# Delta rule with row broadcasts by DMA for tiles 1 to 3, and an earlier square root in the output projections

## The chip, the core and the metric

The kernel runs on one core of a Trainium2 chip. The metric is the device time of one execution in microseconds (us). Five engines work side by side, each in the order of its own program: PE (matmuls), DVE (VectorE), ACT (ScalarE), POOL (GpSimd) and SP (here it only issues DMAs). They meet at semaphores.

## The reference, cut to what matters

The model is a two-layer decoder trunk on 512 tokens of width 1024: one gated-DeltaNet layer, one latent-attention layer, each followed by a mixture of 64 experts with a shared one. The change touches the delta rule of layer 0 and the output projection of both layers, with the norm and the router behind it. The core of the delta rule, per head and chunk of 64 tokens:

```python
g = jnp.cumsum(g, axis=-1)
decay = jnp.exp(jnp.where(incl, g[..., :, None] - g[..., None, :], -jnp.inf))
lower = jnp.where(strict, jnp.einsum('nbhid,nbhjd->nbhij', kb, k) * decay, 0.0)
sol = lax.linalg.triangular_solve(I + lower, rhs, left_side=True, lower=True, unit_diagonal=True)
attn = jnp.einsum('nbhid,nbhjd->nbhij', q, k) * decay
def step(S, inp):                       # scan over the chunks
    v_new = uc - wc @ S
    o = (qc * jnp.exp(gc)[..., None]) @ S + ac @ v_new
    S = S * jnp.exp(g_last)[..., None] + (kc * jnp.exp(g_last - gc)[..., None]).T @ v_new
# after the mixer, in each layer:
h = layer_norm(DN_ALPHA * h + mix, ln1_g[layer], ln1_b[layer])
scores = jax.nn.sigmoid(xf @ w_router)          # first step of the mixture of experts
```

## The kernel before, in words

The delta rule (the block `gdn_delta_rule`) goes over four tiles of 128 tokens, each two chunks. The eight heads are handled as two groups g of four; `s = 2*tt + g` numbers a group of a tile, and nearly all operations are on [128, 4 heads x 128].

For each tile the decay needs the summed gates in two shapes: as a column (one number per partition, `gcol`) and as a row (the same 128 numbers on all partitions). In the same way the weights need `k_gain` as a column and as a row. Rows are made on PE: `gate_rows` (L818) multiplies a broadcast column with the constant triangle `C_CUM`, and `gain_rows` (L837) multiplies a broadcast column with the identity; four matmuls for each group, into PSUM bank 0 or 4.

What happens to them: `decay_arg` (L1013, DVE) subtracts column from row; `decay` (L961, ACT) takes exp of the row twice (`eg_last`, `eg_row`), then abs and exp of the difference, which is `sym`; `upper_part` (L1144, POOL) masks `sym` into `upper`; `keys_queries` (L826, PE) makes key-key and query-key products, two halves for each group; `decayed` (L1018, DVE) multiplies them by `sym` and `upper`; `weighted` (L1028, DVE) multiplies by the gain row and then by the gain column. `diagonal` (L1138, POOL) writes the diagonal of gains into `diag`; `first_X` and `first_Y` (DVE) start the inverse from `diag` and the weighted products.

The triangular solve is an inverse in levels 0 to 4. In each, for both groups, PE makes `product` (L854) and, past level 0, transposes X (L864); ACT copies both to SBUF; PE makes `inverse` (L870); DVE subtracts the result from X. Within the levels of tile tt the rows and products of tile tt+1 are made: `gate_rows` in level 1, `keys_queries` in levels 2 and 3, `gain_rows` in level 4. `decay` of the next tile stands behind ACT's copies of level 2; the squares of the last tile's output (`out_squares`, L1057) stand on DVE behind `decay_arg` in level 1. After level 4 come `values_keys` (L884) and the scan over the tile's two chunks c (`from_state`, `from_values`). The prologue makes the rows and products of tile 0 in one go. Each block ends in a barrier of all engines.

The output projection (`mixer_out`, L1214) runs once in each layer. For each tile of tokens: PE projects, DVE adds the residual and takes the statistics, ACT takes the square root (`act_layer_norm`, L389), DVE normalises in two passes (L386, L387), PE transposes (`pe_rows`), ACT copies the transposed blocks (`act_rows`, L343), and PE computes the router's scores. ACT also rearranges the rows and stores them (`act_store_rows`, L350). The next block, the mixture of experts, begins on ACT with a sigmoid of the router's result (L2116).

Of the kernel before, what the change touches and what calls it, by code (L numbers as in the profile page):

```python
# [33 lines left out]
P = 128  # L34
# [78 lines left out]
def build(nc, a, out):  # L113
    ctx = ExitStack()
    with ctx:
# [14 lines left out]
        moe_sum = nc.dram_tensor("moe_sum", (T, D), F32).ap()  # L130

# [673 lines left out]

        with nc.Block(name="gdn_delta_rule") as block:
            @block.sync
            def _(sp):
                sp.dma_start(onorm[:, :], a["a_onorm_w"][0].rearrange("(p o) -> p o", o=1)).then_inc(onorm_in.sem, 16)

            @block.tensor
            def _(pe):
# [4 lines left out]

                def gate_rows(s):  # L818
                    tt, g, tok, b = tile(s)
                    if tt > 0:  # L820
                        pe.wait_ge(k_scaled.sem, k_scaled.base + s - 1)
                    for h in range(HG):
                        last = nc.tensor.matmul(b[0][:, h * P:(h + 1) * P], lhsT=g_tok[:, tt, HG * g + h:HG * g + h + 1].to_broadcast([P, P]), rhs=plane(C_CUM), start=True, stop=True)
                    last.then_inc(rows_ready.sem, 1)

                def keys_queries(s, half):  # L826
                    tt, g, tok, b = tile(s)
                    if tt > 0 and half == 0:
                        pe.wait_ge(sym_done.sem, sym_done.base + s + 1)
                    elif tt > 0:  # L830
                        pe.wait_ge(kq_done.sem, kq_done.base + ev(s, 0) + 1)
                    for j in range(2):
                        h = HG * g + 2 * half + j
                        last = nc.tensor.matmul(kq_bank(s, half)[:, 2 * j * P:2 * (j + 1) * P], lhsT=qkT[:, H + h, tok], rhs=qk_of[:, :, h, tok], start=True, stop=True)
                    last.then_inc(kq_ready.sem, 1)

                def gain_rows(s):  # L837
                    tt, g, tok, b = tile(s)
                    if tt > 0:
                        pe.wait_ge(kq_done.sem, kq_done.base + ev(s, 1) + 1)  # L840
                    elif g == 0:
# [52 lines left out]
                def from_state(s, c):  # L894
# [30 lines left out]
                for s in both(0):  # L925
                    gate_rows(s)
                for half in range(2):
# [4 lines left out]
                for tt in range(TT):  # L932
                    for level in range(LV):
# [26 lines left out]
            def _(act):  # L960
                def decay(s):  # L961
# [6 lines left out]
                    nc.scalar.activation(eg_last[:, tt % 2, g, :, :], heads(b[0][:, :])[:, :, CHUNK - 1::CHUNK], ACT.Exp)  # L968
                    nc.scalar.activation(eg_row[g][:, :, :], heads(b[0][:, :]), ACT.Exp)
# [7 lines left out]
                nc.scalar.activation(ecol[:, :, :, :], bank[3][:, 0:2 * TT * H].rearrange("p (a t h) -> p a t h", a=2, t=TT), ACT.Exp).then_inc(cols_exp.sem, 1)  # L977
                for s in both(0):
# [33 lines left out]
            def _(v):  # L1012
                def decay_arg(s):  # L1013
                    tt, g, tok, b = tile(s)
                    v.wait_ge(rows_ready.sem, rows_ready.base + s + 1)
                    nc.vector.tensor_tensor(sym[g], heads(b[0][:, :]), per_head(gcol[:, tt, HG * g:HG * g + HG]), ALU.subtract).then_inc(arg_done.sem, 1)
# [11 lines left out]
                def weighted(s):  # L1028
                    tt, g, tok, b = tile(s)
                    v.wait_ge(kq_done.sem, kq_done.base + ev(s, 1) + 1)  # L1030
                    v.wait_ge(b_ready.sem, b_ready.base + s + 1)
                    link(v, "dve", nc.vector.tensor_tensor(sym[g], heads(b_bank(s)[:, :]), S[tt % 2][g][:, :, :], ALU.mult))
# [45 lines left out]
                for tt in range(TT):  # L1078
                    for level in range(LV):
# [7 lines left out]
                        if level == 0:  # L1087
                            for s in both(tt):
# [38 lines left out]
            def _(pool):  # L1127
# [86 lines left out]
        def mixer_out(name, layer, mix_h, mix_l, w_hi):  # L1214
# [35 lines left out]
            with nc.Block(name=name) as block:  # L1250
# [64 lines left out]
                def _(act):  # L1315
# [4 lines left out]
                    for tt in range(TT):  # L1320
# [1158 lines left out]
        for c in (rows_ready, arg_done, sym_done, upper_done, b_ready, w_scaled, ktok_ready, k_scaled, uw_ready):  # L2479
# [133 lines left out]
```

## Time and profile before

| | |
|---|---|
| time, median of 3 runs | 2332.85 us (2330.3 to 2335.3) |
| the profiled execution's own time | 2327.69 us |
| its span | 2325.8 us |
| PE, DVE, ACT, POOL busy, share of the span | 92%, 66%, 56%, 20% |
| mean granted clock of PE, of full speed | 0.959 |
| the delta rule, first to last matmul | 251.2 to 473.5 us |
| end of the output projections, layer 0 and 1 | 551.2 and 1583.5 us |

The span is what the profiler saw of one execution; 1.9 us lie around it. Shares of busy time are means over stages that differ a lot, so the delta rule and the ends of the projections are to be read from their own stretches.

### The profile page before, as it was taken

What the parts mean: (1) busy time and instruction counts of PE and PEld (TensorE: products, weight loads), DVE (VectorE), ACT (ScalarE), POOL (GpSimd) and SP (SyncE); (2) the same over time, 40 slices, a digit from 0 to 9 for tenths busy, and PEclk for the clock granted to TensorE, in tenths of its full rate; (3) what the DMA queues carried; (4) which work ended last, traced back from release to release, by engine and by line L of the source; (5) the groups of instructions that cost most, each with busy time, mean ns of one, the idle gap of its engine ahead of it and who ended that gap; (6) DMA issues with size and microseconds to landing.
All of it is one profiled execution on the core that took longest, in us unless ns stands there. A gap on an engine that the chain in (4) does not pass through costs nothing. (4 is left out here: it accounts for less than half of the span.)

```text
span 2325.8 us, 35565 instructions
## 1 busy us (share of the span) xinstructions
PE 2130.4 (92%) x9937; PEld 1610.7 (69%) x9937; DVE 1542.8 (66%) x2548; ACT 1292.2 (56%) x2140; POOL 475.6 (20%) x367
## 2 busy tenths in 40 slices
PE   7998799999999999999995898998999999999993
PEld 6875688975677767777764745575776676777772
DVE  3762556665688777888774315556777777888884
ACT  3332233433577777777774222332677777777772
POOL 0000355400122222222221003000222222222220
PEclk9999899988999999999998897999999999999997
DMA  5221000004799999999997120026899999999993
GB/s 194 97 90 37 23 1 1 1 28 175 272 370 373 361 360 353 371 362 372 356 352 242 46 68 19 1 86 215 302 340 359 360 354 345 361 361 372 372 360 116
DMA packets 180098, 536.57 MB, mean 231 GB/s; under 512 B 26320, under 2 KB 57904, under 8 KB 180016
## 3 DMA queue, kind: packets, MB, share of 16 engines
q1 hardware_dynamic: 149968, 457.51, 52.3%
q0 software_dynamic: 25248, 69.25, 11.9%
q10 hardware_dynamic: 4800, 8.78, 1.0%
q8 instruction: 45, 0.74, 0.1%
q14 instruction: 37, 0.30, 0.0%
HBM read 501.50 MB, written 54.07 MB: 239 GB/s over the span
## 5 line engine op out<-in xcount | busy, mean ns | idle before, releaser
L1704 DVE TENSOR_TENSOR gu_l<-ring,gu_h 128x1024 fp32r<-128x1024 f32 x512 | 610.5, 1220 | 93.4 <-ACT gu_h L1590 82.9
L1590 ACT CAST gu_h<-ring 128x1024 fp32r<-128x1024 f32 x512 | 523.8, 1060 | 84.8 <-DMA ring<-in_moe_w_up 68.9
L1522 PE MATMUL bank<-gu_h,xgT_l 128*128 128x512 f32 x1024 | 412.8, 403 | 0.0
L1524 PE MATMUL bank<-gu_h,xgT_h 128*128 128x512 f32 x1024 | 401.5, 392 | 0.0
L1523 PE MATMUL bank<-gu_l,xgT_h 128*128 128x512 f32 x1024 | 400.5, 391 | 0.0
L1832 POOL DMA_INDIRECT xg<-h_rows,list_idx x128 | 147.3, 1151 | 911.6 <-issue 523.3
L1561 PE MATMUL bank<-ring,hmT_f 128*128 128x512 f32 x544 | 277.4, 591 | 0.0
L1597 ACT CAST down_h<-ring 128x1024 fp32r<-128x1024 f32 x130 | 136.1, 1047 | 229.9 <-DMA ring<-in_moe_w_down 141.9
L1710 DVE TENSOR_TENSOR down_l<-ring,down_h 128x1024 fp32r<-128x1024 f32 x130 | 159.2, 1225 | 113.0 <-ACT down_h L1597 111.5
L1851 POOL DMA_INDIRECT moe_sum<-y,out_idx x128 | 193.9, 1515 | 167.4 <-issue 144.6
L1524 PEld LDWEIGHTS bank<-gu_h,xgT_h 128*128 128x128 f32 x1024 | 193.0, 188 | 42.5
L1523 PEld LDWEIGHTS bank<-gu_l,xgT_h 128*128 128x128 f32 x1024 | 193.7, 189 | 37.2
L1522 PEld LDWEIGHTS bank<-gu_h,xgT_l 128*128 128x128 f32 x1024 | 193.7, 189 | 36.3
L1692 DVE TENSOR_TENSOR xgT_l<-bank,xgT_h 128x512 fp32r<-128x512 f32 x256 | 164.9, 685 | 43.8 <-ACT xgT_h L1580 35.1
L1558 PE MATMUL bank<-down_h,hmT_l 128*128 128x512 f32 x272 | 163.1, 600 | 6.4 <-DVE hmT_l L1697 6.4
L1496 PE MATMUL bank<-const,xg 128*128 128x128 f32 x1024 | 138.0, 279 | 23.4 <-DMA xg<-h_rows,list_idx 11.4
L1580 ACT CAST xgT_h<-bank 128x512 fp32r<-128x512 f32 x256 | 137.4, 595 | 19.3 <-DVE y L1718 15.6
L1496 PEld LDWEIGHTS bank<-const,xg 128*128 128x128 f32 x1024 | 115.4, 142 | 35.7 <-issue 32.0
L1561 PEld LDWEIGHTS bank<-ring,hmT_f 128*128 128x128 f32 x544 | 102.2, 188 | 23.3
L1534 PEld LDWEIGHTS bank<-const,hm 128*128 128x128 f32 x272 | 34.0, 141 | 111.3 <-DVE hm L1685 79.3
L1560 PE MATMUL bank<-down_h,hmT_h 128*128 128x512 f32 x272 | 106.9, 393 | 0.0
L1559 PE MATMUL bank<-down_l,hmT_h 128*128 128x512 f32 x272 | 106.9, 393 | 0.0
(353 smaller groups left out, 3416.6 us busy)
## 6 DMA issues: line engine op xcount, KB each, us to landing
ring<-in_moe_w_gate SPq DMA_DIRECT2D x256, 512.0 KB
ring<-in_moe_w_up SPq DMA_DIRECT2D x256, 512.0 KB
ring<-in_moe_w_down SPq DMA_DIRECT2D x256, 512.0 KB
ring<-in_a_w_in SPq DMA_DIRECT2D x32, 512.0 KB
ring<-in_a_w_out SPq DMA_DIRECT2D x8, 512.0 KB
h_rows<-ring ACTq DMA_DIRECT2D x8, 512.0 KB, 2.6
moe_sum<-y ACTq DMA_DIRECT2D x8, 512.0 KB, 6.8
ring<-moe_sum SPq DMA_DIRECT2D x8, 512.0 KB, 5.2
```

The costliest lines, as they stand in the source:

```text
L1496: last = nc.tensor.transpose(bank[2 + half][:, j * P:(j + 1) * P], xg[r % 2][:, k * P:(k + 1) * P], ident)
L1522: nc.tensor.matmul(out, lhsT=xl, rhs=wh, start=k == 0, stop=False)
L1523: nc.tensor.matmul(out, lhsT=xh, rhs=wl, start=False, stop=False)
L1524: last = nc.tensor.matmul(out, lhsT=xh, rhs=wh, start=False, stop=k == KD - 1)
L1558: nc.tensor.matmul(out, lhsT=xl, rhs=down_h[:, c], start=True, stop=False)
L1561: last = nc.tensor.matmul(out, lhsT=xf, rhs=ring[:, down_slot, CH + half * 512:CH + half * 512 + 512], start=False, stop=True)
L1590: nc.scalar.copy(gu_h[:, c, :, :], gate_up_cols(gate_slot, c * CH // 2, CH // 2)).then_inc(gu_hi.sem, 1)
L1692: nc.vector.tensor_tensor(xgT_l[:, r % 2, k, :], heads(bank[2 + half][:, :]), xgT_h[:, r % 2, k, :].bitcast(F32), ALU.subtract).then_inc(x ...
L1704: nc.vector.tensor_tensor(gu_l[:, c, :, :], gate_up_cols(gate_slot, c * CH // 2, CH // 2), gu_h[:, c, :, :].bitcast(F32), ALU.subtract).th ...
L1710: nc.vector.tensor_tensor(down_l[:, :], ring[:, down_slot, 0:CH], down_h[:, :].bitcast(F32), ALU.subtract).then_inc(down_lo.sem, 1)
L1832: pool.indirect_dma_start(out=middle_rows(xg[r % 2], n), out_offset=None, in_=h_rows, in_offset=bass.IndirectOffsetOnAxis(ap=list_idx[0:n, ...
L1851: pool.indirect_dma_start(out=moe_sum, out_offset=bass.IndirectOffsetOnAxis(ap=out_idx[0:n, r % 2:r % 2 + 1], axis=0), in_=middle_rows(y[r ...
```

## The change

Three things are changed.

1. The rows of tiles 1 to 3 no longer come from PE. In the prologue eight matmuls (`rows_of_all`) make the gate rows and the gain rows of all four tiles and eight heads once, on 8 partitions; ACT copies them to SBUF in two copies ahead of its first `decay`; SP stores them in a DRAM tensor `gain_row`, and then loads them, 256 KB at a time, broadcast to 128 partitions: gate rows into `upper[g]`, gain rows into `diag[g]` (twelve loads). DVE and ACT read the rows from there. `gate_rows` and `gain_rows` are gone from levels 1 and 4.
2. Waits follow from this. `keys_queries` of the next tile's first half waits for `k_scaled` (level 0) where it waited for `sym_done`, as it does not overwrite a row in the bank any more. `diagonal` on POOL waits for `w_scaled`, since `diag` holds the row until `weighted` has read it. `from_state` waits for the second half of `decayed`. In tile 0 the scaling of the keys waits for the stores, since the rows were copied into a buffer that it writes.
3. In `mixer_out` the square root of the last tile stands ahead of ACT's row copy and store of the tile before, and an added one-element sigmoid stands behind them, ahead of the last `act_rows`.

```diff
+                for kind, rows in enumerate((row_parts, row_parts2)):
+                    sp.wait_ge(row_copied.sem, row_copied.base + kind + 1)
+                    sp.dma_start(gain_row[kind].rearrange("t h q -> h t q"), rows).then_inc(row_stored.sem, 16)
+                sp.wait_ge(row_stored.sem, row_stored.base + 32)
+                for tt in range(1, TT):
+                    for s in both(tt):
...
+                        sp.wait_ge(kq_done.sem, kq_done.base + ev(s - 2, 1) + 1)
+                        sp.dma_start(upper[g], gain_row[0, tt, hs, :].partition_broadcast(P)).then_inc(gate_row_in[g].sem, 16)
+                    for s in both(tt):
...
+                        sp.wait_ge(xy_done.sem, xy_done.base + lev(s - 2, 0, LEVELS) + 1)
+                        sp.dma_start(diag[g], gain_row[1, tt, hs, :].partition_broadcast(P)).then_inc(gain_row_in[g].sem, 16)
...
+                def rows_of_all():
+                    for tt in range(TT):
+                        last = nc.tensor.matmul(bank[2][0:H, tt * P:(tt + 1) * P], lhsT=g_tok[:, tt, :], rhs=plane(C_CUM), start=True, stop=True)
+                    last.then_inc(row_made.sem, 1)
+                    for tt in range(TT):
+                        last = nc.tensor.matmul(bank[6][0:H, tt * P:(tt + 1) * P], lhsT=k_gain[:, tt, :], rhs=ident, start=True, stop=True)
+                    last.then_inc(row_made.sem, 1)
...
                     if tt > 0 and half == 0:
-                        pe.wait_ge(sym_done.sem, sym_done.base + s + 1)
+                        pe.wait_ge(k_scaled.sem, k_scaled.base + s - 1)
+                    elif tt == 0 and half == 1 and g == 0:
+                        pe.wait_ge(row_copied.sem, row_copied.base + 2)
...
-                        pe.wait_ge(w_scaled.sem, w_scaled.base + s + 3)
+                        pe.wait_ge(kq_done.sem, kq_done.base + ev(s + 2, 1) + 1)
...
-                            for s in both(tt + 1):
-                                if level == 1:
-                                    gate_rows(s)
-                                elif level < 4:
-                                    keys_queries(s, level - 2)
-                                else:
-                                    gain_rows(s)
+                            for s in both(tt + 1) if level in (2, 3) else ():
+                                keys_queries(s, level - 2)
...
+                for kind, (rows, b) in enumerate(((row_parts, bank[2]), (row_parts2, bank[6]))):
+                    act.wait_ge(row_made.sem, row_made.base + kind + 1)
+                    nc.scalar.copy(rows, heads(b[0:H, :])).then_inc(row_copied.sem, 1)
...
-                    nc.vector.tensor_tensor(sym[g], heads(b[0][:, :]), per_head(gcol[:, tt, HG * g:HG * g + HG]), ALU.subtract).then_inc(arg_done.sem, 1)
+                    if tt > 0:
+                        v.wait_ge(gate_row_in[g].sem, gate_row_in[g].base + 16 * tt)
...
+                    nc.vector.tensor_tensor(sym[g], upper[g] if tt > 0 else heads(b[0][:, :]), per_head(gcol[:, tt, HG * g:HG * g + HG]), ALU.subtract).then_inc(arg_done.sem, 1)
...
-                    link(v, "dve", nc.vector.tensor_tensor(sym[g], heads(b_bank(s)[:, :]), S[tt % 2][g][:, :, :], ALU.mult))
+                    link(v, "dve", nc.vector.tensor_tensor(sym[g], diag[g] if tt > 0 else heads(b_bank(s)[:, :]), S[tt % 2][g][:, :, :], ALU.mult))
...
-                        pool.wait_ge(xy_done.sem, xy_done.base + lev(s - 2, 0, LEVELS) + 1)
+                        pool.wait_ge(w_scaled.sem, w_scaled.base + s + 1)
...
+                            if tt == TT - 1:
+                                act_layer_norm(act, TT - 1, stats)
                             act_store_rows(act, tt - 1)
-                    act_layer_norm(act, TT - 1, stats)
+                    nc.scalar.activation(stats[0:1, 0, 15:16], eps_col[0:1, 0:1], ACT.Sigmoid)
```

PE's instructions in the prologue before: the gate rows (L823), the products (L834) and the gain rows (L845) of tile 0.

```order
793 L823 MATMUL bank<-const,g_tok 128x128 x8
794 L834 MATMUL bank<-qkT 128x256 x8
795 L845 MATMUL bank<-const,k_gain 128x128 x8
796 L861 MATMUL bank<-X,masked_0 128x128 x4
```

The same place after the change.

```order
793 L850 MATMUL bank<-const,g_tok 128x128 x8
794 L841 MATMUL bank<-const,g_tok 8x128 x4
795 L844 MATMUL bank<-const,k_gain 8x128 x4
796 L863 MATMUL bank<-qkT 128x256 x8
797 L872 MATMUL bank<-const,k_gain 128x128 x8
```

Eight matmuls with 8 output partitions stand between the gate rows and the products.

PE in levels 1 to 4 of tile 0 before, from the inverse of level 1; L861 is `product`, L867 the transpose, L879 and L881 `inverse`, L890 the first of `values_keys`.

```order
804 L879 MATMUL bank<-prod_vnew,Y 128x128 x8
805 L823 MATMUL bank<-const,g_tok 128x128 x8
806 L861 MATMUL bank<-X,masked_0 128x128 x4
...
810 L879 MATMUL bank<-prod_vnew,Y 128x128 x8
811 L834 MATMUL bank<-qkT 128x256 x4
...
822 L881 MATMUL bank<-Y,prod_vnew 128x128 x8
823 L845 MATMUL bank<-const,k_gain 128x128 x8
824 L890 MATMUL bank<-v_tok,Y 128x128
```

The same place after the change.

```order
806 L906 MATMUL bank<-prod_vnew,Y 128x128 x8
807 L888 MATMUL bank<-X,masked_0 128x128 x4
...
811 L906 MATMUL bank<-prod_vnew,Y 128x128 x8
812 L863 MATMUL bank<-qkT 128x256 x4
...
823 L908 MATMUL bank<-Y,prod_vnew 128x128 x8
824 L917 MATMUL bank<-v_tok,Y 128x128
```

The eight matmuls behind level 1 and the eight behind level 4 are gone; the same holds for tiles 1 and 2.

ACT at the end of the output projections before: L352 is the row copy, L353 its store, L391 the square root, L348 the copies of the transposed rows, L2116 the sigmoid of the next block.

```order
252 L348 COPY ring<-bank 128x4x128 x2
253 L352 COPY ring<-ring 128x1024
254 L353 DMA h_rows<-ring 128x1024
255 L391 ACTIVATE ln_stats<-ln_stats,eps_col 128x1
256 L348 COPY ring<-bank 128x4x128 x2
...
261 L2116 ACT_TABLE_LOAD
262 L2116 ACTIVATE scores<-bank 128x256
```

The same place after the change.

```order
253 L349 COPY ring<-bank 128x4x128 x2
254 L392 ACTIVATE ln_stats<-ln_stats,eps_col 128x1
255 L353 COPY ring<-ring 128x1024
256 L354 DMA h_rows<-ring 128x1024
257 L1368 ACT_TABLE_LOAD
258 L1368 ACTIVATE ln_stats<-eps_col 1x1
259 L349 COPY ring<-bank 128x4x128 x2
...
264 L2153 ACTIVATE scores<-bank 128x256
```

The square root has moved ahead of the copy and the store, and the table load from the next block to a place behind them.

## Rows read from the trace of the kernel before

**Rows 1.** Timeline of PE, tile 1: start, us, line, [idle before <- releaser].
```profile
340.48 2.11 PE L879 MATMUL bank<-prod_vnew,Y 128*128 128x128 f32 x16
343.69 1.13 PE L834 MATMUL bank<-qkT 128*128 128x256 f32 x4 [1.10 <-ACT ring L971]
...
346.39 1.05 PE L861 MATMUL bank<-X,masked 128*128 128x128 f32 x8
...
351.00 1.89 PE L834 MATMUL bank<-qkT 128*128 128x256 f32 x8
352.73 1.05 PE L861 MATMUL bank<-X,masked 128*128 128x128 f32 x8
...
357.33 1.95 PE L845 MATMUL bank<-const,k_gain 128*128 128x128 f32 x16
359.12 0.39 PE L890 MATMUL bank<-v_tok,Y 128*128 128x128 f32 x2
```

**Rows 2.** Timeline of PE, tile 0, level 2.
```profile
288.05 2.11 PE L879 MATMUL bank<-prod_vnew,Y 128*128 128x128 f32 x16
...
293.39 1.05 PE L861 MATMUL bank<-X,masked 128*128 128x128 f32 x8
```

**Rows 3.** Timeline of DVE, tile 1, level 1 into level 2.
```profile
336.24 0.69 DVE L1084 TENSOR_TENSOR X<-X,bank 128x512 f32<-128x512 f32 x1 [0.36 <-PE bank L879]
...
338.63 0.68 DVE L1062 TENSOR_TENSOR eg_row<-v_tok 128x512 f32<-128x512 f32 x1
...
341.60 0.68 DVE L1084 TENSOR_TENSOR X<-X,bank 128x512 f32<-128x512 f32 x1
```

**Rows 4.** Timeline of ACT, tile 1, decay of tile 2, first and last operation.
```profile
341.80 0.18 ACT L968 ACTIVATE eg_last<-bank 128x8 f32<-128x8 f32 x1 [0.48 <-DVE o_rms L1064]
...
344.74 0.63 ACT L971 ACTIVATE ring<-ring 128x512 f32<-128x512 f32 x1
```

**Rows 5.** Timelines of PE and ACT in the prologue.
```profile
253.48 3.62 PE L834 MATMUL bank<-qkT 128*128 128x256 f32 x16
...
268.32 2.08 PE L861 MATMUL bank<-X,masked 128*128 128x128 f32 x8 [9.44 <-DVE Y L1047]
...
253.58 0.18 ACT L968 ACTIVATE eg_last<-bank 128x8 f32<-128x8 f32 x1 [0.93 <-DVE ring L1016]
```

**Rows 6.** Timeline of DVE, first_X of tile 0, group 0 beside POOL, group 1 alone.
```profile
261.63 1.63 DVE L1041 TENSOR_TENSOR X<-ring,const 128x512 f32<-128x512 f32 x1
...
269.98 0.69 DVE L1041 TENSOR_TENSOR X<-ring,const 128x512 f32<-128x512 f32 x1
```

**Rows 7.** DMA issues: KB each, median us from issue to landing.
```profile
ln_gain<-in_ln_g SPq DMA_DIRECT2D x4, 512.0 KB, 4.0
```

**Rows 8.** Timelines of DVE, ACT and PE, end of the output projections of layer 0.
```profile
540.70 0.21 DVE L382 BATCH_NORM_AGGREGATE ln_stats<-ln_stats 128x2 f32<-128x12 f32 x1
...
540.06 2.07 ACT L352 COPY ring<-ring 128x1024 f32<-128x1024 f32 x1
...
542.53 0.29 ACT L391 ACTIVATE ln_stats<-ln_stats,eps_col 128x1 f32<-128x1 f32 x1 [0.40 <-ACT ring L352]
546.88 0.58 ACT L348 COPY ring<-bank 128x512 f32<-128x512 f32 x1 [4.05 <-PE bank L340]
...
539.74 2.00 PE L363 MATMUL bank<-ring 128*128 128x64 f32 x16 [0.23 <-ACT ring L348]
545.72 1.97 PE L340 MATMUL bank<-const,ring 128*128 128x128 f32 x8 [3.98 <-DVE ring L387]
547.51 3.68 PE L363 MATMUL bank<-ring 128*128 128x64 f32 x16
```

**Rows 9.** Timelines of ACT and DVE behind the barrier.
```profile
551.48 1.28 ACT L2116 ACT_TABLE_LOAD   x1 [1.19 <-PEq L1250]
...
556.31 0.42 DVE L1747 TENSOR_TENSOR biased<-scores,router_bias 128x256 f32<-128x256 f32 x1 [10.64 <-DMA router_bias<-in_moe_router_bias]
```

**Rows 10.** Timeline of PE, end of the output projections, layer 1.
```profile
1578.05 1.97 PE L340 MATMUL bank<-const,ring 128*128 128x128 f32 x8 [3.98 <-DVE ring L387]
```

More of the change, by code:

```diff
@@ L130, in build @@
         moe_sum = nc.dram_tensor("moe_sum", (T, D), F32).ap()
+        gain_row = nc.dram_tensor("gain_row", (2, TT, H, P), F32).ap()
         const = sb("const", [P, N_CONST, P])
@@ L804, in per_head @@
             return ap.unsqueeze(2).to_broadcast([P, HG, P])
+        row_parts = keg_wT[0][0:H, :, :]
+        row_parts2 = keg_wT[1][0:H, :, :]
+        row_made, row_copied, row_stored = after(convw_ready, 1), after(ab_ready, 1), after(const_in, 16)
+        gate_row_in, gain_row_in = [after(first_half_used, N_QKV), after(v_copied, H)], [after(hT_hi, 2 * TT), after(sums_ready, 2 * H + 1)]
         with nc.Block(name="gdn_delta_rule") as block:
@@ L838, in gain_rows @@
                     tt, g, tok, b = tile(s)
-                    if tt > 0:
-                        pe.wait_ge(kq_done.sem, kq_done.base + ev(s, 1) + 1)
-                    elif g == 0:
+                    if g == 0:
                         pe.wait_ge(cols_exp.sem, cols_exp.base + 1)
@@ L926, in _ @@
                     gate_rows(s)
+                rows_of_all()
                 for half in range(2):
@@ L967, in decay @@
                         act.wait_ge(rms_in.sem, rms_in.base + tt - 1)
-                    nc.scalar.activation(eg_last[:, tt % 2, g, :, :], heads(b[0][:, :])[:, :, CHUNK - 1::CHUNK], ACT.Exp)
-                    nc.scalar.activation(eg_row[g][:, :, :], heads(b[0][:, :]), ACT.Exp)
+                    rows = upper[g] if tt > 0 else heads(b[0][:, :])
+                    nc.scalar.activation(eg_last[:, tt % 2, g, :, :], rows[:, :, CHUNK - 1::CHUNK], ACT.Exp)
+                    nc.scalar.activation(eg_row[g][:, :, :], rows, ACT.Exp)
                     link(act, "act", nc.scalar.activation(sym[g], sym[g], ACT.Abs))
@@ L1014, in decay_arg @@
                     tt, g, tok, b = tile(s)
-                    v.wait_ge(rows_ready.sem, rows_ready.base + s + 1)
-                    nc.vector.tensor_tensor(sym[g], heads(b[0][:, :]), per_head(gcol[:, tt, HG * g:HG * g + HG]), ALU.subtract).then_inc(arg_done.sem, 1)
+                    if tt > 0:
+                        v.wait_ge(gate_row_in[g].sem, gate_row_in[g].base + 16 * tt)
+                    else:
+                        v.wait_ge(rows_ready.sem, rows_ready.base + s + 1)
+                    nc.vector.tensor_tensor(sym[g], upper[g] if tt > 0 else heads(b[0][:, :]), per_head(gcol[:, tt, HG * g:HG * g + HG]), ALU.subtract).then_inc(arg_done.sem, 1)
                 def decayed(s, half):
@@ L1030, in weighted @@
                     v.wait_ge(kq_done.sem, kq_done.base + ev(s, 1) + 1)
-                    v.wait_ge(b_ready.sem, b_ready.base + s + 1)
-                    link(v, "dve", nc.vector.tensor_tensor(sym[g], heads(b_bank(s)[:, :]), S[tt % 2][g][:, :, :], ALU.mult))
+                    if tt > 0:
+                        v.wait_ge(gain_row_in[g].sem, gain_row_in[g].base + 16 * tt)
+                    else:
+                        v.wait_ge(b_ready.sem, b_ready.base + s + 1)
+                    link(v, "dve", nc.vector.tensor_tensor(sym[g], diag[g] if tt > 0 else heads(b_bank(s)[:, :]), S[tt % 2][g][:, :, :], ALU.mult))
                     nc.vector.tensor_tensor(sym[g], sym[g], per_head(k_gain[:, tt, HG * g:HG * g + HG]), ALU.mult).then_inc(w_scaled.sem, 1)
@@ L1087, in _ @@
                         if level == 0:
+                            if tt == 0:
+                                v.wait_ge(row_stored.sem, row_stored.base + 32)
                             for s in both(tt):
@@ L2478, in build @@
         attended_l = sb("attended_l", [P, H, T], F32R, scope=att)
-        for c in (rows_ready, arg_done, sym_done, upper_done, b_ready, w_scaled, ktok_ready, k_scaled, uw_ready):
+        rows_ready.base += 2
+        b_ready.base += 2
+        for c in (arg_done, sym_done, upper_done, w_scaled, ktok_ready, k_scaled, uw_ready):
             c.base += NS
```

6 lines of the change are left out of this document (4 added, 2 removed).

## The prediction

> **What bounds the kernel now.** I read the shares of busy time first (PE 92%, DVE 66%, ACT 56%, POOL 20%), then PE's timeline through the delta rule, then those of DVE, ACT and POOL beside it, and last the ends of the two output projections. In the delta rule PE is the bound nearly everywhere between the prologue and the end. What the reader is to see in [rows 1] is that PE goes from piece to piece without idle time: the products of level 3 run into the next work, the gain rows (L845) into `values_keys` (L890). The only idle time that a row shows is ahead of `keys_queries`, 1.10 us, and ACT's `sym` ends it. So matmuls taken out of the levels should be worth their own length, as long as the engines that feed PE keep up. In the prologue it is otherwise: PE waits 9.44 us for DVE [rows 5], and whatever delays ACT's first `decay` delays all behind it. At the end of the projections PE waits 3.98 us for the norm [rows 8], in both layers [rows 10].
>
> **The change part by part.**
>
> *Rows out of levels 1 and 4.* Sixteen instruction halves for both groups occupy PE for 359.12 - 357.33 = 1.79 us [rows 1]; they last 1.95, so neighbours overlap by 0.16. The gate rows are the same count and form, so also 1.79. In each of tiles 0, 1 and 2 both go.
>
> *The wait for `sym` in level 2.* The inverse of both groups takes 2.11 - 0.16 = 1.95 us of PE [rows 1], one half of the products of the next tile 352.73 - 351.00 = 1.73. Without a wait, level 2's inverse to level 3's first product would thus be 3.68. In tile 0 it is 293.39 - 288.05 = 5.34 [rows 2], in tile 1 346.39 - 340.48 = 5.91 [rows 1]. The new wait, on `k_scaled`, was met a level earlier, so PE gets back 1.66 and 2.23.
>
> *What is late next.* In tiles 1 and 2 DVE also has the squares of the last output here. Before, it starts its second subtraction of level 1 at 336.24, the squares at 338.63, and its first subtraction of level 2 at 341.60, with nothing between [rows 3]. Operations of this size follow each other at some 0.60 us (0.69 less the overlap), so with the gate rows already in SBUF the two `decay_arg` stand at 336.84 and 337.44 and the squares at 338.04: 0.59 earlier, not 1.79. The subtraction then falls at 341.0 and ends at 341.7. PE's level 2 inverse starts at 340.48 - 1.79 = 338.69 and level 3 at 342.37, so the products of the next tile cover this. ACT's `decay` waits for the squares [rows 4]; it moves by the same 0.59 and ends at 344.74 + 0.63 - 0.59 = 344.8. Only then can ACT copy level 3's product and transpose, two copies of 0.6 us: about 345.9. PE would be ready for the inverse at 342.37 + (357.33 - 352.73 - 1.95) = 345.0. That is a new wait of 0.9 us a tile. In tile 0 there are no squares, and the same sum leaves no wait.
>
> Tile 0: 1.79 + 1.66 + 1.79 = 5.2. Tiles 1 and 2: 1.79 + 2.23 + 1.79 - 0.9 = 4.9 each. Together 15.0 us. From below, if DVE and ACT take all of the two row makings back as waits, 15.0 - 6 x 1.79 = 4.3; from above, if the new wait doesn't come, 16.8.
>
> *The prologue.* Eight matmuls with 8 output partitions stream the same 128 columns, so I take the same 1.79 us for them. They push the products from 253.48 to 255.3 [rows 5]. ACT makes two copies of 512 columns (0.58 each, by the row for such a copy [rows 8]); the second can start about 0.25 after its matmuls, at 255.5, and `decay` starts at 256.05 in place of 253.58: +2.5 us. From there to PE's first product of level 0 all is one chain through ACT, POOL and DVE. Bounds: 0, if the rows cost PE and ACT nothing, and +3.5, if both copies lie wholly behind the matmuls and the first product finds PE's clock low for a little longer.
>
> *The DMAs.* Two stores and twelve loads on SP, whose queue has nothing else here but one small load. A load of 512 KB broadcast to 128 partitions lands after 4.0 us [rows 7]; these have 256 KB. The gate rows of tile 2, say, are sent for when the second half of `decayed` of tile 1 is over (before 303 us) and are wanted at 336.8. The first, of tile 1, are sent for once the prologue has read `upper` (about 263) and wanted at 286.8. I cost them at 0; behind the wait on them DVE's subtractions queue, so a late one would cost what it is late, up to the whole. The wait on the stores in level 0 is met some 20 us earlier, 0.
>
> *POOL and DVE.* `diagonal` now waits for `weighted`, and so works while DVE handles the other group and, later, `first_X`. Beside a busy POOL such an operation of DVE took 1.63 us, alone 0.69 [rows 6]. The change also turns `decay_arg` and the first step of `weighted` into operations with two inputs in SBUF. If both steps of `first_X` were hit in three tiles and lay on the path, 6 x 0.94 = +5.6; below, 0. I take 0, because PE has `values_keys` and the state products to do between, and keep 5.6 for the range. The Trainium skill (SBUF — State Buffer, "Who interferes with whom") says that a DVE instruction with two SBUF inputs contends with a GpSimd instruction that reads SBUF, and that the one that comes second blocks fully. The pair in [rows 6] agrees in kind. By that rule the change adds 12 exposed operations where before there was a PSUM input; that is the slower rival below.
>
> *The square root.* The statistics of the last tile are ready at 540.70 + 0.21, the root starts at 542.53, behind the row copy (2.07) and its store [rows 8]. Moved ahead it starts at 541.0: 1.5 us earlier, and with it DVE's two passes and PE's transposes. The copy, the store (0.4), the table load (1.28, [rows 9]) and the one-element sigmoid (0.2) then fill ACT from 541.25 to 545.2; the transposed rows come at 546.88 - 1.5 = 545.4. It fits with 0.2 us to spare. Twice 1.5 = 3.0. Bounds 0 and 3.2 at PE's present clock.
>
> *The table load* saved behind the barrier: 0. DVE's first routing step starts at 556.31 and waits for the DMA of the router's bias, not for the scores, which were there at 553.2 [rows 9].
>
> The Trainium skill (ScalarE: Activation LUTs, "What ACT_TABLE_LOAD costs") puts a drain of about 1.38 us beside each switch, 2.66 in all. [rows 9] show 1.28 with the barrier ahead and no such drain. By that rule the filled wait would overrun by 1.2 us and leave 0.3 of the 1.5 in each layer, a total of 13.2 in place of 15.5.
>
> **The sum.** -15.0 + 2.5 - 3.0 = -15.5 us. On the profiled execution: 2327.69 - 15.5 = 2312.2. Its time is 5.2 below the median of the runs and below all three of them, so I put the change on the median: 2332.85 - 15.5 = 2317.3, say 2317. What lies behind, the experts, starts after a barrier each time and only shifts.
>
> **The rivals.**
>
> *The feeding engines take the room (smaller gain).* PE's idle time ahead of `keys_queries` shows that ACT is already late once a tile, and DVE's row of squares has no gap [rows 3]. Against it: at the other places no idle row of PE stands. With all six row makings back as waits: -4.3 + 2.5 - 3.0 = -4.8, 2328. Halfway, some 2323.
>
> *Contention turns it slower.* One mechanism: between level 4 and the state's update POOL is busy later than before, and DVE's operations with two SBUF inputs stretch by 0.94 each. In tiles 1 to 3 there are 6 `decay_arg`, 12 in `weighted`, 12 in `first_X`: 30 x 0.94 = 28 us, giving 2345. It decides from the 17th stretched operation that lies on the path (16 us). For it: [rows 6]. Against it: POOL is busy only 20% of the span, and PE has other work where these run.
>
> *PE's clock holds at the ends (more gain).* Behind the 3.98 us wait the router's 16 instructions take 3.68 us, where they took 2.00 a tile earlier [rows 8], the lower clock level by its ratio. With a wait of 2.5 us it may stay high: 1.7 in the router and 0.9 in the transposes, of which ACT's own copies and store give back about half. Some 1.3 a layer, -18, 2315. The other way round, a longer idle time in the prologue can leave the low level on for 1 to 2 us more.
>
> *The rows come late.* A landing 20 us longer than the row would be needed; I give it no weight of its own.
>
> **How the numbers follow.** Forecast, 2312 to 2322: 0.65. The clock holds or the new wait doesn't come, 2309 to 2315: 0.10. Half the gain is taken back by waits, contention or the overrun on ACT, 2322 to 2327: 0.13. All six row makings come back as waits, 2328 and about: 0.07. Slower by contention: 0.05. A measurement of this kernel tells about 0.2% (4.7 us) from no change, so faster means under 2328.2: 0.65 + 0.10 + 0.13 = 0.88; same 0.07; slower 0.05. The range 2310 to 2326 leaves out the last two cases and the outer edges.
>
> **What would show it.** Right: no idle time of PE ahead of `keys_queries` in level 2; a wait of some 0.9 us ahead of level 3's inverse in the tiles of level 2 with squares, ended by ACT; level 0's first product about 2.5 us later; the delta rule 12.5 us shorter; the last square root within 0.2 us of the statistics and the barrier 1.5 us earlier in both layers. Wrong: DVE idle on a DMA of `gain_row`; `first_X` at 1.6 us with PE idle behind it; ACT's table load ending after the transposes; the routing starting no earlier.

## The result, and the profile after

The changed kernel took 2308.9 us (median of 4 runs, 2305.9 to 2311.1) against 2332.3 (4 runs, 2330.3 to 2335.3): ratio 0.9897, 95% interval 0.9879 to 0.9915, or 23.4 us less. The forecast was 15.5 less, 2317, with a range from 2310 to 2326. Two later comparisons of the same pair on other chips gave 0.9936 (0.9916 to 0.9956) and 0.9904 (0.9882 to 0.9926). The single times of the two kernels in all comparisons together are 16 of the changed one with mean 2310.1 and 64 of the one before with mean 2329.9: 19.8 us less, with a standard error of 1.0 worked out from their scatter. Single runs of the kernel before lie between 2322.9 and 2337.3.

The profiled execution took 2311.05 us, its span is 2309.3 (before 2325.8): 16.5 less, where 15.5 had been worked out. The page shows 9857 matmuls in place of 9937 (96 taken out, 16 put in).

PE, tile 1, levels 1 to 3 of the changed kernel, from the timeline (start, us, line, [idle time before <- what ended it]); it answers to [rows 1]:

```profile
333.12 1.06 PE L888 MATMUL bank<-X,masked 128*128 128x128 f32 x8
...
335.78 2.11 PE L906 MATMUL bank<-prod_vnew,Y 128*128 128x128 f32 x16
337.73 1.89 PE L863 MATMUL bank<-qkT 128*128 128x256 f32 x8
339.46 1.05 PE L888 MATMUL bank<-X,masked 128*128 128x128 f32 x8
...
343.13 2.10 PE L906 MATMUL bank<-prod_vnew,Y 128*128 128x128 f32 x16 [0.85 <-ACT Y L1015]
```

`keys_queries` (L863) is one piece of eight without idle time; from the inverse of level 2 (335.78) to the first product of level 3 (339.46) it is 3.68 us, the sum made beforehand, where before it was 5.91. The new wait ahead of level 3's inverse is there, 0.85 us, and ACT ends it. PE's waits on ACT in the delta rule, whole stage; first the kernel before, then the changed one (line, what it waited for, us in total, times, longest):

```profile
PE bank L834 <- ACT ring L971: 4.5, 6, 1.1
```

```profile
PE bank L906 <- ACT Y L1015: 1.7, 2, 0.9
```

What is late next, from DVE's timeline of the changed kernel; it answers to [rows 3]:

```profile
333.32 0.69 DVE L1117 TENSOR_TENSOR X<-X,bank 128x512 f32<-128x512 f32 x1 [0.36 <-PE bank L906]
333.93 1.29 DVE L1046 TENSOR_TENSOR ring<-ring,gcol 128x512 f32<-128x512 f32 x2
335.13 0.68 DVE L1095 TENSOR_TENSOR eg_row<-v_tok 128x512 f32<-128x512 f32 x1
...
338.10 1.28 DVE L1117 TENSOR_TENSOR X<-X,bank 128x512 f32<-128x512 f32 x2
```

and ACT's, which answers to [rows 4]:

```profile
338.30 0.21 ACT L992 ACTIVATE eg_last<-ring 128x8 f32<-128x8 f32 x1 [1.68 <-DVE o_rms L1097]
...
341.40 0.63 ACT L995 ACTIVATE ring<-ring 128x512 f32<-128x512 f32 x1
```

The two `decay_arg` run together right behind the subtraction, neither waits for a DMA, and the squares follow them: ACT's `decay` waits for DVE's squares and not for a row.

The prologue, PE, ACT and SP; it answers to [rows 5]:

```profile
253.64 1.04 PE L841 MATMUL bank<-const,g_tok 128*8 128x128 f32 x8
254.52 1.04 PE L844 MATMUL bank<-const,k_gain 128*8 128x128 f32 x8
255.49 3.72 PE L863 MATMUL bank<-qkT 128*128 128x256 f32 x16
270.81 2.07 PE L888 MATMUL bank<-X,masked 128*128 128x128 f32 x8 [9.81 <-DVE Y L1080]
```

```profile
255.59 0.57 ACT L1004 COPY keg_wT<-bank 8x512 f32<-8x512 f32 x1 [0.30 <-PE bank L844]
256.08 0.16 ACT L992 ACTIVATE eg_last<-bank 128x8 f32<-128x8 f32 x1
```

```profile
255.32 1.15 SPq L817 DMA_DIRECT2D gain_row<-keg_wT  x2
262.17 0.95 SPq L824 DMA_DIRECT2D ring<-gain_row  x2
298.73 1.19 SPq L824 DMA_DIRECT2D ring<-gain_row  x2
```

The 16 instructions with 8 output partitions take 255.49 - 253.64 = 1.85 us (1.79 assumed); ACT starts `decay` at 256.08 (256.05 expected), and the first product falls at 270.81, 2.49 behind [rows 5]. SP sends for the gate rows of tile 2 at 298.7; DVE reads them at 333.9.

The end of the projections in layer 0, first ACT, then PE, then DVE behind the barrier; it answers to [rows 8] and, with the scores, to [rows 9]:

```profile
529.42 0.29 ACT L392 ACTIVATE ln_stats<-ln_stats,eps_col 128x1 f32<-128x1 f32 x1 [0.77 <-DVE ln_stats L383]
529.62 2.05 ACT L353 COPY ring<-ring 128x1024 f32<-128x1024 f32 x1
...
532.06 1.28 ACT L1368 ACT_TABLE_LOAD   x1 [0.39 <-ACT ring L353]
533.35 0.20 ACT L1368 ACTIVATE ln_stats<-eps_col 1x1 f32<-1x1 f32 x1
533.76 0.58 ACT L349 COPY ring<-bank 128x512 f32<-128x512 f32 x1 [0.21 <-PE bank L341]
538.38 0.38 ACT L2153 ACTIVATE scores<-bank 128x256 f32<-128x256 f32 x1 [1.19 <-PEq L1285]
```

```profile
532.61 1.97 PE L341 MATMUL bank<-const,ring 128*128 128x128 f32 x8 [2.39 <-DVE ring L388]
534.40 3.68 PE L364 MATMUL bank<-ring 128*128 128x64 f32 x16
```

```profile
542.65 0.42 DVE L1784 TENSOR_TENSOR biased<-scores,router_bias 128x256 f32<-128x256 f32 x1 [10.10 <-DMA router_bias<-in_moe_router_bias]
```

PE's wait has shrunk from 3.98 to 2.39 us. The root stands right behind the statistics; copy, store, table load and sigmoid end at 533.55, and ACT then waits 0.21 us for the transposed rows: everything fits, with the 0.2 to spare that was worked out. The sigmoid starts 0.01 us behind the end of the table load. The Trainium skill (ScalarE: Activation LUTs, "What ACT_TABLE_LOAD costs") adds a drain to each switch; here no row has room for one, and the sum without it was right. Behind the barrier the routing still starts with the router's bias.

Where the time went, by stages, as means over the profiles (four of the kernel before, three of the changed one; us):

| Stage | before | changed | difference | forecast |
|---|---|---|---|---|
| up to the delta rule | 250.9 | 251.0 | 0.0 | 0 |
| delta rule | 225.4 | 212.4 | -13.0 | -12.5 |
| from there to the barrier, layer 0 | 76.0 | 73.8 | -2.3 | -1.5 |
| experts, attention, to the barrier of layer 1 | 1030.8 | 1027.8 | -3.0 | -1.5 |
| to the end | 742.8 | 741.8 | -1.0 | 0 |
| span | 2326.0 | 2306.7 | -19.3 | -15.5 |

### The profile page after: what moved, and what is told of

Read it like the earlier page. It is cut to its first block and busy times, and to the rows that moved or that the text cites. A ratio compares the mean times of both kernels' runs of the same rounds, so it can differ in the third digit from the quotient of the medians.

```text
span 2309.3 us, 35424 instructions
## 1 busy us (share of the span) xinstructions
PE 2121.8 (92%) x9857; PEld 1603.3 (69%) x9857; DVE 1548.1 (67%) x2548; ACT 1293.9 (56%) x2144; POOL 485.6 (21%) x367
## 5 line engine op out<-in xcount | busy, mean ns | idle before, releaser
L1888 POOL DMA_INDIRECT moe_sum<-y,out_idx x128 | 198.7, 1553 | 172.6 <-issue 148.0
L1561 PEld LDWEIGHTS bank<-gu_h,xgT_h 128*128 128x128 f32 x1024 | 193.0, 189 | 42.5
L1598 PEld LDWEIGHTS bank<-ring,hmT_f 128*128 128x128 f32 x544 | 102.5, 188 | 23.4
```

Of the source, the lines that this page charges most:

```text
L1561: last = nc.tensor.matmul(out, lhsT=xh, rhs=wh, start=False, stop=k == KD - 1)
L1598: last = nc.tensor.matmul(out, lhsT=xf, rhs=ring[:, down_slot, CH + half * 512:CH + half * 512 + 512], start=False, stop=True)
L1888: pool.indirect_dma_start(out=moe_sum, out_offset=bass.IndirectOffsetOnAxis(ap=out_idx[0:n, r % 2:r % 2 + 1], axis=0), in_=middle_rows(y[r ...
```

## The experiments

**Changed kernel, again.** No edit.

> The changed kernel once more, unaltered. Theory A (my steps hold, and the rest of the 23.4 us is how executions of one kernel spread, since the profiled execution of before stood 5 us under its own median and that of the changed kernel 2 us above its own): ratio about 0.9925, near the 16.5 us by which the two spans differ; the profile again shows the first product of level 0 2.5 us later than before, the first transpose of the output projections 11.6 us earlier and the router's barrier of layer 0 13.1 us earlier. Theory B (a lasting gain that my steps do not hold, in the experts or the attention): ratio again 0.990, and a stage of the profile behind layer 0's router more than 5 us shorter than before.

Measured: 2312.4 us (6 runs) against 2327.8 (23 runs), 0.9936 (0.9916 to 0.9956): 15.4 less. The first comparison's 23.4 is not a size that repeats to the microsecond.

**The delta rule's edits alone.** The end of `mixer_out` as before.

```diff
-                            if tt == TT - 1:
-                                act_layer_norm(act, TT - 1, stats)
                             act_store_rows(act, tt - 1)
-                    nc.scalar.activation(stats[0:1, 0, 15:16], eps_col[0:1, 0:1], ACT.Sigmoid)
+                    act_layer_norm(act, TT - 1, stats)
```

> Only the delta rule's part of the change; the square root and the table load stand as before. Theory A: 11.5 to 12.5 us faster than before (0.995). Theory B with the gain tied to the new DRAM tensor or to the loads: some 18 to 20 us faster (0.992).

Measured: 2314.0 (6 runs) against 2327.8, 0.9942 (0.9921 to 0.9964). The delta rule has the length of the changed kernel (first product to the first transpose of its output 193.0 us, as there), and from there to the barrier it is 76.1 us, as before: PE waits 3.98 us for the norm again. The delta rule's edits carry most of the gain: 13.8 of the 15.4 us that the whole change has against the same runs.

**The output projection's edits alone.** The delta rule as before, the end of `mixer_out` as changed.

> Only the output projections' part: the square root of the last tile ahead of the row copy, the sigmoid's table loaded during the wait; the delta rule as before. Theory A: 3 us faster (0.9987), barrier 1.5 us earlier in each layer. Theory B with the gain tied to the table load or to when the experts' loads start: 6 to 10 us faster.

Measured: 2329.1 (12 runs) against 2327.8, 0.9999 (0.9985 to 1.0014). As a time this is inconclusive: the interval holds no change, and 3 us less (0.9987) as well. The profile shows them: PE's wait is 2.39 in place of 3.98. The stage takes 74.5 us to the barrier; it took 74.8 to 77.4 in four profiles of before, a scatter in which 1.5 us would not be seen.

**The kernel before, as a new run.** No edit; it is a yardstick for what such a comparison can tell.

> The kernel before, unaltered, timed against itself: how far executions of one kernel lie apart. Theory A: ratio 1.000 with single times from 2327 to 2335, and a profiled span that can lie several us off the median. Theory B: single times within 2 us and the span at its median, so that the 23.4 us are real in full.

Measured: 1.0016 (1.0001 to 1.0032) for a kernel against itself, 2331.1 (12 runs) to 2327.8. Its profile brought what the prediction lacked. PE in level 2 of tile 1, then the same stretch by windows (busy us of PE, weight loads, DVE, ACT, POOL, then the granted clock, DMA share, GB/s):

```profile
344.59 1.13 PE L834 MATMUL bank<-qkT 128*128 128x256 f32 x4 [1.10 <-ACT ring L971]
346.32 1.92 PE L834 MATMUL bank<-qkT 128*128 128x256 f32 x4 [0.60 <-ACT ring L971]
348.03 1.91 PE L861 MATMUL bank<-X,masked 128*128 128x128 f32 x8
```

```profile
344.00:348.00 4.00, 2.81 (x8) 2.02 (x9) 0.96 (x3) 2.24 (x5) 2.48 (x2) 0.81 0.01 2
```

In the execution that the prediction was made from, the waits end 0.9 us earlier. It has, in the same window:

```profile
344.00:348.00 4.00, 3.40 (x23) 2.86 (x22) 1.60 (x4) 1.86 (x5) 3.16 (x3) 1.00 0.01 2
```

Behind the same waits of 1.10 and 0.60 us PE was granted half its clock (1.2 in place of 2.4 GHz; "half clock" from here on) for some 3.4 us: the second four products took 1.92 in place of 1.13, the eight behind them 1.91 in place of 1.06. The same happened in tile 2, and at the border of tiles 0 and 1. The stage took 212.0 us from first product to transpose, where it had taken 207.1. In the run with the projection's edits alone it happened in tiles 1 and 2 (210.6).

**Changed kernel, a third time.** No edit, on another chip.

> The changed kernel once more, on whichever chip comes. Two comparisons so far: 4 executions against 4 gave -23.4 us, 6 against 23 gave -15.4. Theory A (sampling: executions of each kernel lie within some 12 us, and four against four fell on the far side): again some -15 to -17 us, ratio near 0.993, with the two intervals meeting. Theory B (it depends on the chip or the hour, with the change worth 23 us in one place): a ratio near 0.990 in at least one further comparison.

Measured: 2310.0 (6 runs) against 2331.2 (11 runs), 0.9904 (0.9882 to 0.9926), 21.2 less.

**The rows of all tiles made later in the prologue**, behind the products and gain rows of tile 0, ACT's copies behind the decays.

```diff
-                    elif tt == 0 and half == 1 and g == 0:
-                        pe.wait_ge(row_copied.sem, row_copied.base + 2)
...
-                rows_of_all()
...
+                pe.wait_ge(kq_done.sem, kq_done.base + 4)
+                rows_of_all()
```

> The eight matmuls that make the rows of all tiles move behind the prologue's other matmuls (once the second half of the decayed products has freed their banks), and ACT's two copies behind both decays. My theory of the prologue's +2.5 us (the copies stand ahead of ACT's decay): the first product of level 0 comes 2.5 us earlier than with the change, at the same place as before, the loads still land more than 10 us ahead of their readers, and the whole is 2 to 3 us faster than the changed kernel, 18 us faster than before. Rival (the later first product came from something else, or later rows arrive too late): first product unchanged, or DVE idle on a DMA in level 1 of tile 0.

Measured: 2309.8 (6 runs), 0.9903 (0.9881 to 0.9925), not to be told from the changed kernel. In the profile ACT's `decay` starts, and PE's first product with it, where they do in the kernel before:

```profile
253.05 0.18 ACT L991 ACTIVATE eg_last<-bank 128x8 f32<-128x8 f32 x1 [0.93 <-DVE ring L1045]
```

```profile
267.81 2.08 PE L886 MATMUL bank<-X,masked 128*128 128x128 f32 x8 [6.09 <-DVE Y L1079]
```

From the start of the stage (250.65) that is 17.16 us, against 19.57 in the changed kernel and 17.15 before. So the prologue's term is shown in the profile, cause and size: 2.4 us for rows ahead of the decays. It is too small for the times.

**The router's bias loaded a stage early.**

```diff
+                    sp.dma_start(router_biases[layer][:, :], a["moe_router_bias"][layer].partition_broadcast(P)).then_inc(bias_in.sem, 16)
```

> The changed kernel with the router's bias loaded in the block of the output projections, in both layers, where it came behind the barrier. The routing on DVE can then start with the scores, some 3.9 us earlier in layer 0 and 3 us in layer 1. Theory 1 (PE is busy with the shared expert until after the first gather has landed, so the routing is off the path): the routing starts 3 to 4 us earlier, the first gathered rows are transposed at the same time after the barrier, and the time stays within 1 us of the changed kernel. Theory 2 (the routing is the path behind the barrier): 6 to 8 us faster than the changed kernel.

Measured: 2312.8 (4 runs), 0.9916 (0.9888 to 0.9944). The routing now starts with the scores, 4.0 us earlier:

```profile
538.69 0.42 DVE L1786 TENSOR_TENSOR biased<-scores,router_bias 128x256 f32<-128x256 f32 x1 [6.31 <-ACT scores L2154]
579.42 1.04 PE L1535 MATMUL bank<-const,xg 128*128 128x128 f32 x8
```

PE's first transposes of gathered tokens stand at 579.42; in the changed kernel they stand at 580.26. Of the 4.0 us 0.8 is left there, and none in the time. Counted from the router's last matmul the first transposes come after 41.5 us, where they come after 42.2, 41.9 and 41.8 in the three profiles of the changed kernel, so 0.3 to 0.7 us is the better figure. So the saved table load is hidden twice, by the bias and by what lies between the routing and the experts.

**Both together.**

> Both of the last two edits together on the changed kernel. By my theories 2.5 us faster than the changed kernel by the prologue alone, some 18 us faster than before; by the rival on the routing some 24 us.

Measured: 2308.7 (6 runs, 2302.6 to 2317.5), 0.9911 (0.9886 to 0.9935). It has the shortest span of all profiles (2300.7) and the lowest median, but it can't be told from the changed kernel.

**The wait for `sym` put back**, in the changed kernel, all else left.

```diff
                     if tt > 0 and half == 0:
+                        pe.wait_ge(sym_done.sem, sym_done.base + s + 1)
                         pe.wait_ge(k_scaled.sem, k_scaled.base + s - 1)
```

> The changed kernel, with one wait put back: the next tile's first half of keys_queries again waits for sym_done, as before, besides k_scaled. Theory C (the part of the gain that my sum lacks is PE's clock: the waits of PE in level 2 of the kernel before are followed, in some executions, by a stretch at half the granted clock that costs 1.7 us each, and the profiled execution of before happened to have none): the waits of PE ahead of keys_queries come back, 0.5 to 1.1 us each, the stage from the first product of level 0 to the output projections grows from 193 us by 4 to 6 us of waiting, and low stretches behind those waits appear in part of the executions. About 5 to 8 us slower than the changed kernel. Rival D (the clock's stretches have nothing to do with those waits): 4 to 6 us slower, and no low stretch behind them in any profile.

Measured: 2321.9 (9 runs, 2319.0 to 2324.7) against 2329.1 (14 runs), 0.9968 (0.9956 to 0.9981). It keeps 7.2 us of the gain of 19.8 (4.4 to 10.2 by the interval), and so loses some 12.6 by this one wait, where the expectations were 5 to 8 and 4 to 6. PE, then the waits of the stage and two windows:

```profile
341.93 1.10 PE L864 MATMUL bank<-qkT 128*128 128x256 f32 x4 [2.47 <-ACT ring L996]
343.74 2.02 PE L864 MATMUL bank<-qkT 128*128 128x256 f32 x4 [0.70 <-ACT ring L996]
345.55 1.84 PE L889 MATMUL bank<-X,masked 128*128 128x128 f32 x8
```

```profile
PE bank L864 <- ACT ring L996: 7.3, 6, 2.5
```

```profile
344.00:348.00 4.00, 4.00 (x20) 3.64 (x20) 0.76 (x2) 0.58 (x2) 3.72 (x3) 0.60 0.01 2
396.00:400.00 4.00, 3.77 (x21) 3.44 (x22) 1.50 (x4) 0.77 (x3) 3.72 (x3) 0.70 0.00 0
```

With the gate rows' matmuls gone, PE comes to the wait earlier and stands there for 7.3 us in all, not 4.5. Both level 2 waits have a stretch of half clock behind them, and one more stands at the border of tiles 2 and 3. From first product to transpose it is 202.7 us against 193.0. Of the 9.7 us 7.3 - 1.7 = 5.6 are waits and some 2 x 1.7 the stretches in level 2: 9.0. The stretch at a border adds nothing, since the 193.0 have one too. The rest fits what a wait costs beside its idle time, because the work around it no longer runs as one piece: in tile 0, at full clock there, level 2's inverse to level 3's first product takes 5.54 us, 1.86 more than the 3.68 without a wait, for 1.38 us of idle time. The other 3 us of the time aren't located; the interval is as wide.

**The same, a second profile.**

> The same kernel, one more profile, to count low stretches of the granted clock behind PE's waits in level 2. Theory C: one or two in the tiles with squares, in at least one of the two profiles. Rival D: none.

Measured: the stage takes 202.8 us, with the clock at 0.60 and 0.70 in the same two windows. The waits of 2.5 us were followed by half clock in four cases of four. Its span is 6.0 longer than that of the run above (2326.1), with the same delta rule: that difference arose in the experts and the attention.

**The kernel before, two more profiles.**

> The kernel before, one more profile. Theory C: the stage from the first product of level 0 to the output projections takes 207.1 us plus 1.7 for each low stretch in it, most of them behind the waits of level 2; of three such profiles so far one had none, one two, one three. Rival D: the stretches lie elsewhere.

> The kernel before, a last profile for the same count. Theory C as in the look ahead of this one: 207 to 213 us for the stage, low stretches behind PE's waits of level 2.

Measured: 206.97 us in both, with the clock full in level 2. Of the five profiles of that delta rule three show no such stretch (207.1, 207.0, 207.0), two show it in both tiles (212.0, 210.6). So it is two executions of five rather than four independent cases of ten. Among the seven profiles of kernels without the wait (192.2 to 193.0 us) none has one in level 2; five have one at the border of tiles 1 and 2. Two of five against none of seven could be chance; with the long waits it is two executions of two.

## Why the prediction was right or wrong

**The mechanism of the delta rule was right, term by term.** Each tile from its first product to that of the next, before and changed in the profiled pair: tile 0 57.57 to 52.18, so -5.4 (forecast -5.2); tile 1 53.00 to 48.21, -4.8 (-4.9, with the new wait of 0.9, measured 0.85); tile 2 53.00 to 49.07, -3.9 (-4.9), and 48.20 in the third profile of the changed kernel. The 0.9 between those two is a stretch of half clock at the border of tiles 1 and 2:

```profile
371.19 3.87 PE L888 MATMUL bank<-X,masked 128*128 128x128 f32 x16 [0.37 <-DVE state L1154]
```

Tile 3 is 43.55 in both. The prologue cost +2.4, as forecast. Together the pair's delta rule is 11.7 shorter, where 12.5 was forecast. That the pair's spans still differ by 16.5, near the 15.5, is partly luck: its experts and attention came out 3.7 us shorter, where 1.5 was forecast, and that stage scatters by more.

**The rival of contention was seen, and lay off the path.** In the changed kernel, over tiles 1 to 3 (DVE by line, count, busy us, mean ns, idle time before):

```profile
L1075 DVE TENSOR_TENSOR X<-ring,X 128x512 f32<-128x512 f32 x6 | 9.8, 1640 | 0.2
...
L1066 DVE TENSOR_TENSOR ring<-ring,k_gain 128x512 f32<-128x512 f32 x6 | 6.3, 1052 | 0.2
...
L1046 DVE TENSOR_TENSOR ring<-ring,gcol 128x512 f32<-128x512 f32 x6 | 3.9, 685 | 0.0
```

Against before (1165 and 692 ns for the same steps) that is 2.9 and 2.2 us more on DVE, and nothing on `decay_arg`. The prediction named two ways to it: POOL is busy at a later time, and 12 operations get a second input in SBUF, `decay_arg` and the first step of `weighted` (L1065). Only the first came. None of the 12 was stretched, and in no `decay_arg` of tiles 1 to 3 was POOL at work. What was stretched, the second step of `weighted` (L1066) and `first_X`, had both inputs in SBUF before; new is that POOL's `diagonal` (L1177) and what follows it now run beside more of them. DVE and POOL behind level 4 of tile 0:

```profile
305.35 0.69 DVE L1065 TENSOR_TENSOR ring<-ring,S 128x512 f32<-128x512 f32 x1
305.51 1.42 POOL L1177 TENSOR_TENSOR ring<-const,k_gain 128x512 f32<-128x512 f32 x1 [8.57 <-DVE ring L1066]
306.07 1.41 DVE L1066 TENSOR_TENSOR ring<-ring,k_gain 128x512 f32<-128x512 f32 x1
```

None of it ends a wait of PE that was not there before; PE has the state's products to do. Of the 30 operations that the rival counted on, 12 were stretched (all six of the last step of `first_X`, three of its first step, three in `weighted`'s second step), and six of those in `first_X` had been before. The feeding engines took no row back either, but for the one wait that was forecast.

**The ends were right in kind.** Root and barrier came 1.5 us earlier. The rival that PE's clock holds there came true in part: in layer 1 the transposes behind the shorter wait start at full clock and take 1.2 to 1.4 us, not 1.97, in all three profiles of the changed kernel, though the router behind them is at half clock each time:

```profile
1561.58 1.16 PE L341 MATMUL bank<-const,ring 128*128 128x128 f32 x8 [2.40 <-DVE ring L388]
1563.04 3.67 PE L364 MATMUL bank<-ring 128*128 128x64 f32 x16 [0.30 <-ACT ring L349]
```

The router follows 1.46 us behind the start of the transposes in place of 1.80 (the wait before is in [rows 10]), 0.3 us earlier where the rival had 1.3, and in layer 0 nothing. That what lies behind the barrier "only shifts" was wrong in layer 1. From the router's last matmul to the first transposes of gathered tokens it is 41.5 to 41.7 us in the four profiles of before and 42.5 to 42.6 in the three of the changed kernel, since half clock now lasts 6 us behind that matmul in place of 4. It goes with the projection's edits: 42.5 with them alone, 41.6 with the delta rule's alone. Some 0.9 us of the 1.8 gained there is lost again. A slip in the prediction's own sum changes nothing: the overrun on ACT that it prices for the drain would leave 13.1 in total, not 13.2.

**What failed: the price of the wait for `sym`, and PE's clock, which the sum holds constant.** The step "PE gets back 1.66 and 2.23" read the wait from one execution in which nothing followed it. In two of five profiles PE's clock fell to half behind it in tiles 1 and 2, 1.7 us each time (the tile takes 54.67 in place of 53.00). The mean length of that stage before is therefore 208.7 us and not the 207.1 of the profile used, and the level term is -15.9 on the means of five and seven profiles (192.8 against 208.7), where it was -15.0 in the sum and -14.1 in the pair. Putting the wait back shows the mechanism with its sign: four stretches of four, in the same place, though behind longer waits.

This covers about 1 of the 4.3 us between the forecast of -15.5 and the -19.8 of all runs. More of it goes with the clock in the rest of the execution, for which the sum has no term. The record has the span and the mean granted clock of every run of these comparisons but four, and span x (1 - clock) is what half clock would cost if it always cost its full price. It is 98.8 us on average over 60 runs of the kernel before and 95.4 over the 16 of the changed one: 3.5 less, with a standard error of 1.0. Without it the spans are 2229.1 and 2213.0, so 16.1 less, with an error of 0.8, beside the forecast of 15.5. Among the 60 runs a microsecond of it goes with 0.7 us of span, so 2.4 to 3.5 of the 19.8 us go with the clock. This is an estimate from a correlation; only the part in level 2, 1.4 us of these, was put to a test by an edit.

**What is not explained.** Why the changed kernel spends less time at half clock outside level 2 stays open, and so do the 1 to 2 us that are left; the 19.8 itself has a standard error of 1.0. By the table of stages they lie in the projections and behind them, where single profiles of one kernel differ as much. The stage to the barrier took 77.4 and 74.8 us in two profiles of the kernel before, the longer one with half clock for 23 us in it and the shorter with 17. Experts and attention took from 1025.5 us, with 94 at half clock (both late edits together), to 1036.9, with 126 (the wait put back, second profile). The range was too narrow at its lower end, by 1.1 us in the first comparison: it had been made from the unknowns of the sum, around a median of three runs, and a comparison of a few runs of this kernel with a few others is itself unsure by some 4 us. That first comparison gave the largest gain of the three.

## What to carry to other kernels

A wait on PE costs its own length, a little for the broken run of work around it and, in some executions, half clock behind it; price it from several profiles, and count a wait removed as worth more than its row shows. When matmuls ahead of a wait are taken out, the wait grows by what they took, so moving the rows to DMA paid in full only because the wait went too. When an operation is stretched by a neighbour, look at which engine works beside it at that moment, and not only at where its inputs lie. Build a sum on a single profile if it is sound, but place it by the scatter of single runs, not by the interval of its own terms.

## What the runs showed of the hardware

- A wait of PE of 1.1 us and one of 0.6 us a little later were followed by about 3.4 us at half the granted clock in 4 of 10 cases (both tiles 1 and 2 in two of five profiles), the same program and the same waits each time; a wait of 2.5 us in 4 of 4; without a wait there, in 0 of 14. In level 2 such a stretch cost 1.7 us, at the border of two tiles 0.9, since PE otherwise waits 0.7 us there.
- A matmul of 128 columns with 8 output partitions takes as long as one with 128: 16 instructions in 1.85 us against 1.79.
- The 256 KB broadcasts from DRAM to 128 partitions landed a median of 3.2 us after their issue.
- ACT's table load took 1.28 us with nothing behind it: the next activation started 0.01 us later.
- A DVE operation of 128x512 f32 with both inputs in SBUF took 0.69 us with POOL idle and up to 1.74 beside it. In tiles 1 to 3: the last step of `first_X` 1.64 in six of six (POOL at work throughout), the second step of `weighted` 1.41 in three and 0.69 in the three with POOL idle, `decay_arg` 0.69 in six of six, all with POOL idle.
- Time at half clock differs between executions of one kernel: the mean granted clock of the kernel before lay between 0.953 and 0.961, and a microsecond of span x (1 - clock) went with 0.7 us of span.
